# A fused two-block transformer kernel: the order of the down products' matmuls in three of four feed-forward groups

## The chip, the cores and the metric

The kernel runs on one NeuronCore of a Trainium2 chip. The metric is device time in microseconds (us) of one launch; lower is better. The engines run side by side and meet only at semaphores: TensorE multiplies into PSUM, VectorE and ScalarE compute element by element, GpSimd does so on SBUF only, and SyncE issues most of the transfers from HBM. PSUM has eight banks, each of 128 x 512 numbers of 32 bit.

## The reference

Two transformer blocks on 512 tokens of width 1024, one after the other, all in float32. The first one ends in the feed-forward network that this case is about:

```python
def first_block(x, ln1_w, w_in, ..., w_out, ln2_w, w_up, w_down):
...
    h = h + mix @ w_out[l]
    hn = rms_norm(h, ln2_w[l])
    h = h + jnp.square(jax.nn.relu(hn @ w_up[l])) @ w_down[l]
    return h
```

Here `w_up` is 1024 x 4096 and `w_down` 4096 x 1024. The second block (adaptive norms, an mLSTM and an S5 mixer, a gated feed-forward network) starts from its result.

## The kernel before

**Numbers in two parts.** Every matmul operand in float32 is split into a high part and the rest (`hi`, `lo`), and a product is three matmuls into the same bank: hi x hi, hi x lo, lo x hi (lines 445 to 447 and 495 to 497).

**The weight stream.** All weights come in one stream of tiles of 16 blocks of 128 x 128 (1 MB each). SyncE loads a tile into one of two `raw` slots as soon as GpSimd is done with the tile two before it. ScalarE copies it to one of two `whi` slots (line 984) once the last chunk that reads the old tile in that slot is finished: `hi_upto` waits for a semaphore of TensorE. GpSimd then computes `wlo` = `raw` - `whi` in four quarters (line 1504) and counts each in `lo_split`. TensorE waits for `lo_split` before the first use of a quarter. ScalarE, GpSimd and SyncE take the tiles strictly in the order of the stream.

**The feed-forward network.** The 4096 hidden channels go in four groups, `for g, kg in enumerate(FF1_GROUPS)`, of eight blocks of 128 channels each. For each group TensorE first makes eight up products (`gemm("up{g}.{j}")`, line 445 ff., 24 matmuls each, two products from one weight tile), in the two G banks in turn. ScalarE takes each out with a Relu; VectorE squares it and splits it into `Bhi[:, j]` and `Blo[:, j]` (lines 2114 to 2118) and signals `B_ready`. Then comes the down product `token_gemm("dn{g}")`, which adds the group's share to the 512 x 1024 result X. It needs four weight tiles and 192 matmuls of 128 x 512:

- First half: columns 0 to 511. The 512 tokens are four token tiles i = 0 to 3, one sum in one of the four T banks each. Tile one of the weights holds blocks k = 0 to 3 of the channels, tile two k = 4 to 7. The order is block by block: for each k the three matmuls of all four token tiles.
- Second half: columns 512 to 1023, again four sums, in the banks G0, G1, O0, O1, and again two weight tiles. The order is the table `staggered` of pairs (weight tile q, token tile i): 12 matmuls each, three pairs of the first weight tile ahead of the first pair of the second, and the last of the first tile's pairs in fifth place.

When a token tile's sum is done (`done`), VectorE adds the bank to X (`add_token`, line 1591), which frees the bank. A group's up products 0 and 1 use banks G0 and G1, thus they wait for the additions of the sums (half 1, token tiles 0 and 1) before them. The first tile of a half releases its `whi` slot when its last matmul is done (`full_W0`), the second one when the half's last sum is done.

**What else VectorE does there.** In the first three groups it also multiplies rows of the adaptive-norm weights (`adaw`, line 1905, 48 pieces, loaded by SyncE in turn with the weight tiles), and it prepares tables of the S5 mixer in small pieces (`s5_piece`) between the additions of the two halves.

**The other order.** `token_gemm` has a switch `by_rows`. With it the second weight tile of the first half, and both of the second half, run token tile by token tile. Before, the mixer's product in the second block uses it for all of its width, and the last group of the second feed-forward network does.

Of the kernel before, what the change touches and what calls it, by code (L numbers as in the profile page):

```python
# [164 lines left out]
def build(nc, d, out):  # L165
    ctx = ExitStack()
    with ctx:
# [16 lines left out]
        def at(name, shape, off, dt=F32):  # L184
            return nc.alloc_sbuf_tensor_at(name, shape, dt, offset=off)
# [14 lines left out]
        Bhi, Blo = at("Bhi", [P, 8, S], offB, F32R), at("Blo", [P, 8, S], offB + 16384, F32R)  # L200
# [218 lines left out]
        def _(pe):  # L419
# [30 lines left out]
            def gemm(name, hi, lo):  # L450

                ps, where = bank("G")
                done(blocks_of(ps, name, hi, lo, range(CHUNKS[INDEX[name]][1])), name, where)

            def gemm_pair(names):

                two = [bank("G") for _ in names]
                for k in range(DC):
                    pe.wait_ge(sem("A_ready"), T.due("A_ready"))
                    for name, (ps, where) in zip(names, two):  # L460
                        ins = blocks_of(ps, name, Ahi, Alo, [k])
                        if k == DC - 1:
                            done(ins, name, where)
# [8 lines left out]
            def normed_rows(s):  # L472

                eight = {}
                for i in range(NT):
                    pe.wait_ge(sem("norm_rows"), T.due("norm_rows"))
                    for k in range(DC) if i else (0, 1, 4, 5, 6, 7, 2, 3):
                        if i == 0:
                            eight[k] = bank("GGOOTTTT"[k])
                        ps, where = eight[k]  # L480
                        ins = pe.transpose(ps[:, i * P:(i + 1) * P], N[:, i, k * P:(k + 1) * P], ident)
                        if i == NT - 1:
                            done(ins, f"xT{s}.{k}", where)
# [301 lines left out]
            for g, kg in enumerate(FF1_GROUPS):  # L785
                for j in range(kg):
                    if g == 0 and j == 0:
                        gemm_pair(["up0.0", "up0.1"])
                    elif g or j > 1:
                        gemm(f"up{g}.{j}", Ahi, Alo)  # L790
                token_gemm(f"dn{g}", Bhi, Blo, kg, "B_ready")
            normed_rows(2)


# [1937 lines left out]
```

## Time and profile before

| | us |
|---|---|
| median of 3 runs | 1525.86 |
| lowest and highest run | 1524.65, 1527.56 |
| the profiled execution, time | 1520.88 |
| the profiled execution, span from first to last instruction | 1519.1 |
| mean granted TensorE clock in it, of full speed | 0.987 |

The profile is of one execution. Its rows are counted in us from the first instruction; lines are those of the kernel file. A matmul's row gives a modelled duration that overlaps the next matmul's, so what TensorE takes is read from start to start. PE is TensorE's matmuls, PEld its weight loads, DVE is VectorE, ACT is ScalarE, POOL is GpSimd. The first feed-forward network lies between about 340 and 690 us: group 0's down product starts at about 381, group 1's at 478, group 2's at 567 and group 3's at 656 us.

### The profile page before, as it was taken

Reading aid. Unit: us, or ns where it says so; the run is one execution under the profiler, and the core shown is the slowest. Engines: PE = TensorE matmul, PEld = TensorE weight load, DVE = VectorE, ACT = ScalarE, POOL = GpSimd, SP = SyncE. Lnnn points to the kernel's source line nnn. Section 1 sums busy time; section 2 is a strip of 40 time slices with the busy share of each in tenths; the row PEclk is TensorE's granted clock in tenths of the full one; section 3 lists DMA queues with packets and bytes.
Section 4 is the critical chain, followed back from the end, with each engine's and each line's share of the span. In section 5 each row is a group of like instructions: output and inputs, shape, how many; then the busy total and the mean of one; then the engine's idle time right before and its main releaser. Section 6 shows DMA issues by size and latency. Waiting matters only on the chain.

```text
span 1519.1 us, 19247 instructions
## 1 busy us (share of the span) xinstructions
PE 1454.3 (96%) x7136; PEld 1172.8 (77%) x7136; DVE 890.4 (59%) x1454; ACT 566.3 (37%) x742; POOL 685.9 (45%) x520
## 2 busy tenths in 40 slices
PE   6999999999999999998999999999988999999997
PEld 4777766778888787887888777778867888888886
DVE  4773557557857788877491556355675333332357
ACT  5233467443222121225342755544335231332231
POOL 2442145426465455654461424445533445354553
PEclk9999999999999999999899999999998999999999
DMA  7323030025646454233734433243213232223222
GB/s 314 111 70 118 29 112 2 29 92 205 243 161 235 152 194 153 84 111 104 161 127 135 171 112 132 104 181 126 106 46 138 83 111 93 102 83 111 83 83 83
DMA packets 48324, 185.69 MB, mean 122 GB/s; under 512 B 12976, under 2 KB 14256, under 8 KB 33392
## 3 DMA queue, kind: packets, MB, share of 16 engines
q1 hardware_dynamic: 30384, 165.53, 30.8%
q10 hardware_dynamic: 17856, 19.01, 4.5%
q8 instruction: 57, 0.93, 0.2%
q14 instruction: 27, 0.22, 0.0%
HBM read 169.71 MB, written 12.58 MB: 120 GB/s over the span
## 4 chain that ended last, share of the span: by engine, by line
issue 32%; PE 26%; POOL 24%; DVE 2%; ACT 0%; POOLq 0%; DVEq 0%
POOL wlo L1504 23%; PE bank L445 5%; PE bank L446 5%; PE bank L447 5%; PE bank L495 3%; PE bank L497 3%; PE bank L496 3%; PE bank L692 1%; DVE X L2393 0%; PE bank L469 0%; PE bank L763 0%; DVE X L2405 0%; POOL wlo L1512 0%; DVE st L1544 0%; DVE X L1591 0%
## 5 line engine op out<-in xcount | busy, mean ns | idle before, releaser
L1504 POOL TENSOR_TENSOR wlo<-raw,whi 128x512 fp32r<-128x512 f32 x440 | 632.8, 1469 | 763.6 <-ACT whi L984 763.5
L445 PE MATMUL bank<-Ahi,whi 128*128 128x512 f32 x1088 | 437.1, 402 | 14.1 <-DVE Alo L1638 4.4
L446 PE MATMUL bank<-Alo,whi 128*128 128x512 f32 x1088 | 426.8, 392 | 0.0
L447 PE MATMUL bank<-Ahi,wlo 128*128 128x512 f32 x1088 | 426.8, 392 | 0.0
L984 ACT ACTIVATE whi<-raw 128x2048 fp32r<-128x2048 f32 x113 | 216.5, 1916 | 239.9 <-PE bank L497 214.0
L445 PEld LDWEIGHTS bank<-Ahi,whi 128*128 128x128 f32 x1088 | 206.3, 190 | 66.1 <-issue 9.7
L447 PEld LDWEIGHTS bank<-Ahi,wlo 128*128 128x128 f32 x1088 | 206.2, 189 | 44.1
L446 PEld LDWEIGHTS bank<-Alo,whi 128*128 128x128 f32 x1088 | 206.5, 190 | 43.5 <-issue 2.4
L495 PE MATMUL bank<-whi,Bhi 128*128 128x512 f32 x496 | 193.9, 391 | 1.7 <-DVEq L1871 1.7
L497 PE MATMUL bank<-whi,Blo 128*128 128x512 f32 x496 | 193.7, 390 | 0.0
L496 PE MATMUL bank<-wlo,Bhi 128*128 128x512 f32 x496 | 193.5, 390 | 0.0
L495 PEld LDWEIGHTS bank<-whi,Bhi 128*128 128x128 f32 x496 | 93.5, 188 | 21.4 <-issue 1.9
L497 PEld LDWEIGHTS bank<-whi,Blo 128*128 128x128 f32 x496 | 93.4, 188 | 19.6
L496 PEld LDWEIGHTS bank<-wlo,Bhi 128*128 128x128 f32 x496 | 93.5, 189 | 19.4
L2449 DVE TENSOR_SCALAR FG<-GP,par 128x512 f32<-128x512 f32 x22 | 12.9, 585 | 130.5 <-ACT GP L1485 130.5
L1905 DVE CUSTOM_DVE_ANT_0 junk<-adaw,cB 128x1024 f32<-128x1024 f32 x48 | 76.9, 1601 | 21.1 <-DMA adaw<-in_ada 16.1
L1208 ACT ACTIVATE G<-bank 128x512 f32<-128x512 f32 x32 | 19.2, 599 | 123.6 <-PE bank L447 123.5
L2114 DVE TENSOR_TENSOR G<-G 128x512 f32<-128x512 f32 x32 | 36.7, 1147 | 31.5 <-ACT G L1208 31.0
L1521 POOL TENSOR_SCALAR Pr<-Pr,MX,GT 128x384 f32<-128x384 f32 (+3 forms) x64 | 37.3, 594 | 31.8 <-DVE MX L1839 31.7
L1591 DVE TENSOR_TENSOR X<-X,bank 128x512 f32<-128x512 f32 x48 | 33.0, 688 | 29.8 <-PE bank L497 28.3
L1485 ACT ACTIVATE GP<-bank 128x512 f32<-128x512 f32 x22 | 13.2, 599 | 98.5 <-PE bank L447 98.4
L1389 ACT ACTIVATE stage<-bank,par 128x512 f32<-128x512 f32 x32 | 21.9, 684 | 66.1 <-PE bank L447 59.0
(397 smaller groups left out, 1872.8 us busy)
## 6 DMA issues: line engine op xcount, KB each, us to landing
raw<-in_ws SPq DMA_DIRECT2D x113, 1024.0 KB, 5.0
adaw<-in_ada SPq DMA_DIRECT2D x48, 512.0 KB, 4.7
spill<-stage ACTq DMA_DIRECT2D x32, 256.0 KB, 2.0
X<-in_x SPq DMA_DIRECT2D x8, 512.0 KB, 5.9
gates<-spill SPq DMA_DIRECT2D x16, 256.0 KB, 5.4
w1k<-in_w1k SPq DMA_DIRECT2D x1, 2048.0 KB, 15.9
w1v<-in_w1v SPq DMA_DIRECT2D x1, 2048.0 KB, 20.1
XM<-spill ACTq DMA_DIRECT2D x8, 256.0 KB, 3.3
```

What stands on the lines that cost most here:

```text
L445: pe.matmul(ps[:], wh, hi[:, k], start=(k == 0), stop=False)
L446: pe.matmul(ps[:], wh, lo[:, k], start=False, stop=False)
L447: ins = pe.matmul(ps[:], wl, hi[:, k], start=False, stop=(k == kn - 1))
L495: pe.matmul(ps[:], h, wh, start=(k == 0), stop=False)
L496: pe.matmul(ps[:], h, wl, start=False, stop=False)
L497: return pe.matmul(ps[:], l, wh, start=False, stop=stop)
L984: act.activation(whi[n % 2][:], raw[n % RAW][:], ACT.Copy).then_inc(sem("hi_split"), 1)
L1504: pool.tensor_tensor(wlo[slot][:, part], raw[slot][:, part], rd(whi[slot][:, part]), ALU.subtract).then_inc(sem("lo_split"), 1)
L1521: pool.tensor_scalar(Pr[u % RING][:, 0:n], Pr[u % RING][:, 0:n], MX[:, u:u + 1], GT[:, i, g:g + 1], ALU.mult, ALU.mult).then_inc(sem("p_re ...
L1591: ins = tt(x, x, ps[:], ALU.add)
L1905: dve.tensor_tensor_reduce(junk[:], adaw[t % 3][:], cB[:], 1.0, 0.0, ALU.mult, ALU.add, mod[:, t:t + 1]).then_inc(sem("ada_used"), 1)
L2114: tt(r[:], r[:], r[:], ALU.mult).then_inc(sem("dve_step"), 1)
```

## The change

Groups 0, 1 and 2 call the down product with `by_rows`; group 3 does not.

```diff
@@ -788,7 +788,7 @@
                         gemm_pair(["up0.0", "up0.1"])
                     elif g or j > 1:
                         gemm(f"up{g}.{j}", Ahi, Alo)
-                token_gemm(f"dn{g}", Bhi, Blo, kg, "B_ready")
+                token_gemm(f"dn{g}", Bhi, Blo, kg, "B_ready", by_rows=g < 3)
             normed_rows(2)
```

Only TensorE's instructions move. In the second half of group 0's down product, these are the places where bank or weight tile changes, with the waits (bank 0 and 1 are G0 and G1, bank 6 and 7 are O0 and O1; `whi0` is the slot of the half's first weight tile, `whi1` of its second; each row stands for 12 matmuls but the first three of a pair that wait, which stand for 3). Before, on TensorE:

```order
L495 MATMUL bank0<-whi0_51,Bhi_57 128x512 [waits free_O1,free_O0,lo_split,free_G1,free_G0]
...
L495 MATMUL bank1<-whi0_51,Bhi_57 128x512
...
L495 MATMUL bank6<-whi0_51,Bhi_57 128x512
...
L495 MATMUL bank0<-whi1_52,Bhi_57 128x512 [waits lo_split]
...
L495 MATMUL bank7<-whi0_51,Bhi_57 128x512
...
L495 MATMUL bank1<-whi1_52,Bhi_57 128x512
...
L495 MATMUL bank6<-whi1_52,Bhi_57 128x512
...
L495 MATMUL bank7<-whi1_52,Bhi_57 128x512
...
L445 MATMUL bank0<-Ahi_55,whi0_51 128x512 [waits lo_split,free_G0]
```

The same place now:

```order
L495 MATMUL bank0<-whi0_51,Bhi_57 128x512 [waits free_O1,free_O0,lo_split,free_G1,free_G0]
...
L495 MATMUL bank0<-whi1_52,Bhi_57 128x512 [waits lo_split]
...
L495 MATMUL bank1<-whi0_51,Bhi_57 128x512
...
L495 MATMUL bank1<-whi1_52,Bhi_57 128x512
...
L495 MATMUL bank6<-whi0_51,Bhi_57 128x512
...
L495 MATMUL bank6<-whi1_52,Bhi_57 128x512
...
L495 MATMUL bank7<-whi0_51,Bhi_57 128x512
...
L495 MATMUL bank7<-whi1_52,Bhi_57 128x512
...
L445 MATMUL bank0<-Ahi_55,whi0_51 128x512 [waits lo_split,free_G0]
```

The first use of `whi1` has moved from behind 36 matmuls to behind 12, and the last use of `whi0` from the 60th matmul to the 84th of 96; the last two rows are the half's end and the next group's first up product.

In the first half of the same product, with the second weight tile, the banks of the four sums are 3, 4, 5, 2. Before, on TensorE, from that tile's first matmul on:

```order
L495 MATMUL bank3<-whi1_52,Bhi_57 128x512 [waits B_ready,lo_split]
...
L495 MATMUL bank4<-whi1_52,Bhi_57 128x512
...
L495 MATMUL bank5<-whi1_52,Bhi_57 128x512
...
L495 MATMUL bank2<-whi1_52,Bhi_57 128x512
...
L495 MATMUL bank3<-whi1_52,Bhi_57 128x512 [waits B_ready,lo_split]
```

The same place now:

```order
L495 MATMUL bank3<-whi1_52,Bhi_57 128x512 [waits B_ready,lo_split]
L496 MATMUL bank3<-wlo1_54,Bhi_57 128x512
L497 MATMUL bank3<-whi1_52,Blo_58 128x512
L495 MATMUL bank3<-whi1_52,Bhi_57 128x512 [waits B_ready,lo_split]
...
L495 MATMUL bank4<-whi1_52,Bhi_57 128x512
```

The second wait for B and weights comes after 3 matmuls where it came after 12; all four of them now stand in the first token tile's 12 matmuls.

## Rows read from the trace of the kernel before

**Rows 1.** page, part 1: busy time (us), share of the span, instructions

```profile
PE 1454.3 (96%) x7136; PEld 1172.8 (77%) x7136; DVE 890.4 (59%) x1454; ACT 566.3 (37%) x742; POOL 685.9 (45%) x520
```

**Rows 2.** instructions in order of time, TensorE: start, us, engine, line, operation

```profile
391.46 0.39 PE L495 MATMUL bank<-whi,Bhi 128*128 128x512 f32 x1
...
402.34 0.39 PE L495 MATMUL bank<-whi,Bhi 128*128 128x512 f32 x1
...
489.38 0.39 PE L495 MATMUL bank<-whi,Bhi 128*128 128x512 f32 x1
...
512.62 0.50 PE L445 MATMUL bank<-Ahi,whi 128*128 128x512 f32 x1 [1.31 <-DVE X L1591]
...
578.02 0.39 PE L495 MATMUL bank<-whi,Bhi 128*128 128x512 f32 x1
...
601.90 0.50 PE L445 MATMUL bank<-Ahi,whi 128*128 128x512 f32 x1 [1.96 <-DVE X L1591]
```

**Rows 3.** the same view, ScalarE, group 0; idle time before in brackets

```profile
402.60 1.92 ACT L984 ACTIVATE whi<-raw 128x2048 fp32r<-128x2048 f32 x1 [8.96 <-PE bank L497]
...
416.22 1.92 ACT L984 ACTIVATE whi<-raw 128x2048 fp32r<-128x2048 f32 x1 [2.52 <-PE bank L497]
```

**Rows 4.** the same view, GpSimd: four subtractions of one tile in a row

```profile
404.59 5.79 POOL L1504 TENSOR_TENSOR wlo<-raw,whi 128x512 fp32r<-128x512 f32 x4 [4.86 <-ACT whi L984]
...
470.30 7.98 POOL L1504 TENSOR_TENSOR wlo<-raw,whi 128x512 fp32r<-128x512 f32 x4 [4.42 <-ACT whi L984]
...
491.63 5.02 POOL L1504 TENSOR_TENSOR wlo<-raw,whi 128x512 fp32r<-128x512 f32 x4 [5.70 <-ACT whi L984]
...
580.28 5.07 POOL L1504 TENSOR_TENSOR wlo<-raw,whi 128x512 fp32r<-128x512 f32 x4 [5.86 <-ACT whi L984]
...
602.03 5.03 POOL L1504 TENSOR_TENSOR wlo<-raw,whi 128x512 fp32r<-128x512 f32 x4 [1.91 <-ACT whi L984]
```

**Rows 5.** waits, 340 to 720 us: us in total, times, longest

```profile
PE bank L445 <- DVE X L1591: 3.3, 2, 2.0
```

**Rows 6.** in order of time, VectorE, the first feed-forward network

```profile
387.11 1.66 DVE L2118 TENSOR_TENSOR Blo<-G,Bhi 128x512 fp32r<-128x512 f32 x1
...
411.71 2.86 DVE L1591 TENSOR_TENSOR X<-X,bank 128x512 f32<-128x512 f32 x4
...
511.87 2.85 DVE L1591 TENSOR_TENSOR X<-X,bank 128x512 f32<-128x512 f32 x4
...
601.16 2.85 DVE L1591 TENSOR_TENSOR X<-X,bank 128x512 f32<-128x512 f32 x4
...
678.47 0.69 DVE L1591 TENSOR_TENSOR X<-X,bank 128x512 f32<-128x512 f32 x1 [4.06 <-PE bank L497]
```

**Rows 7.** in order of time, the mixer's product, which runs row by row

```profile
1097.38 0.39 PE L495 MATMUL bank<-whi,Ahi 128*128 128x512 f32 x1
...
1108.27 0.39 PE L495 MATMUL bank<-whi,Ahi 128*128 128x512 f32 x1
...
1108.52 1.92 ACT L984 ACTIVATE whi<-raw 128x2048 fp32r<-128x2048 f32 x1 [8.96 <-PE bank L497]
...
1110.52 4.99 POOL L1504 TENSOR_TENSOR wlo<-raw,whi 128x512 fp32r<-128x512 f32 x4 [5.86 <-ACT whi L984]
...
1111.85 0.50 PE L495 MATMUL bank<-whi,Ahi 128*128 128x512 f32 x1 [0.70 <-POOL wlo L1504]
...
1115.57 0.50 PE L495 MATMUL bank<-whi,Ahi 128*128 128x512 f32 x1 [0.27 <-POOL wlo L1504]
```

**Rows 8.** page, part 6: DMA issues, KB each, median us to landing

```profile
raw<-in_ws SPq DMA_DIRECT2D x113, 1024.0 KB, 5.0
```

**Rows 9.** stretches: us, busy of PE, PEld, DVE, ACT, POOL, granted clock, DMA, GB/s

```profile
511.10:512.60 1.50, 0.20 (x1) 0.00 (x0) 1.33 (x6) 1.20 (x1) 0.00 (x0) 1.00 0.62 131
1108.20:1132.50 24.30, 22.77 (x97) 17.56 (x97) 18.16 (x35) 11.27 (x14) 4.99 (x4) 1.00 0.03 13
724.00:734.00 10.00, 10.00 (x64) 9.96 (x64) 7.69 (x5) 2.95 (x4) 9.15 (x5) 0.69 0.38 133
```

## The prediction

> **What bounds the kernel now.** TensorE is busy 96% of the span [rows 1], so I read its own row of time first. In the first feed-forward network its matmuls start 226.7 ns apart: 48 of them lie between 391.46 and 402.34 us, 10.88 / 48 [rows 2]. One weight tile feeds 48 matmuls, so it lasts 10.88 us. The engines behind it have slack: the copy to `whi` takes 1.92 us on ScalarE [rows 3], the four subtractions of `wlo` 5.0 to 8.0 us on GpSimd [rows 4]. The reader is to see in rows 3 and 4 not how long these take but when they may start: `whi` has two slots, and the copy starts 0.26 us after the last matmul that reads the old tile (402.60 against 402.34) [rows 2, 3]. GpSimd begins 1.99 us after the copy did (404.59) [rows 4].
>
> The other thing to see is who keeps TensorE waiting now. In the whole network it waits twice for VectorE's additions to X at an up product [rows 5], for bank G0. Unhindered, the second half of a down product lasts 96 x 0.2267 = 21.76 us. So group 1 would have gone on at 489.38 + 21.76 = 511.14 and went on at 512.62: 1.48 us lost. Group 2: 578.02 + 21.76 = 599.78 against 601.90: 2.12 us lost [rows 2]. Together 3.60 us. VectorE was not waiting for TensorE there. Its four additions run back to back from 511.87 and from 601.16, the first ending at 512.56 and 601.85, because other work of its own came before them [rows 6].
>
> **The change, part by part.** Only TensorE's order changes, in three down products, and no instruction is added or removed.
>
> *First half, second tile.* Block by block becomes token tile by token tile. The waits for blocks 4 to 7 of B and of the weights now fall within 21 matmuls, less than 5 us, instead of 37 matmuls. In group 1 the last quarter of that tile is ready at 470.30 + 7.98 = 478.28 [rows 4], before the tile is begun (489.38 - 10.88 = 478.50). In group 0 the last B ends at 387.11 + 1.66 = 388.77 [rows 6], before 391.46. So this costs nothing: the cover is 0.2 us plus the 9 matmuls (2.04 us) until block 7 is due. Three of four sums are finished up to 8 us sooner, but VectorE begins these additions only at 411.71 in group 0, 9.4 us after the half has ended at 402.34, and is late in the other groups too, where even the second half's additions start after their sums [rows 2, 6]. I put that at nothing.
>
> *Second half, second tile.* Before, three token tiles of the first weight tile (36 matmuls, 8.16 us) stood ahead of the first use of the second. Now 12 matmuls stand there, 2.72 us. The slot of the second tile is freed only at the end of the first half, in both orders, since the last bank of that half ends there. Then block 7 is wanted 12 + 9 = 21 matmuls after the half began, 4.76 us, and is there 0.06 us after GpSimd's pass ends. From rows 2 and 4:
> group 0: 404.59 + 5.79 + 0.06 = 410.44, wanted 402.34 + 4.76 = 407.10, wait 3.34 us;
> group 1: 491.63 + 5.02 + 0.06 = 496.71, wanted 494.14, wait 2.57 us;
> group 2: 580.28 + 5.07 + 0.06 = 585.41, wanted 582.78, wait 2.63 us.
> Together 8.54 us. The kernel has one product in this very order, the mixer's. Its second half starts at 1108.27, ScalarE copies at 1108.52, GpSimd passes from 1110.52 for 4.99 us, and block 7 starts at 1115.57 where 1113.03 was due: 2.54 us late, in four waits [rows 7]. The 0.06 us is from there (1110.52 + 4.99 = 1115.51).
>
> *The next group's first up product.* Its tile takes the slot of the half's first tile, which is released by that tile's last matmul: before after 60 of 96 matmuls (copy at 416.22, and 402.34 + 13.60 = 415.94) [rows 2, 3], now after 84. Then 12 matmuls, 2.72 us, are left. From the release to the first usable quarter the mixer shows 1111.85 - 1108.27 = 3.58 us [rows 7]. Wait 0.86 us, three times 2.58 us. The later quarters come every 1.25 us and are used every 2.72 us. If VectorE shares the pass, a quarter can take 2.0 us (7.98 / 4) instead of 1.25 [rows 4], and each wait is 1.6 us. I take 0.86, because the pass that runs beside the additions at 601.16 takes 5.03 us [rows 4, 6], and these additions are what lies beside it.
>
> *The lost 3.60 us.* TensorE now reaches the next up product at 511.14 + 2.57 = 513.71 and 599.78 + 2.63 = 602.41 on the old scale, after bank G0 was freed at 512.56 and 601.85. Both waits for VectorE vanish. They don't come on top but are replaced: the gain is 3.60 us, and what is late next is the weight tile.
>
> *What else moves.* The third tile after the half is fetched when GpSimd's pass over the up tile ends. That pass ends about 4 us after the up product starts, not before it. The load lands 5.0 us later [rows 8]; with up to 7 us it is there about when its slot comes free (10.88 us), and it is not read for another 10.88 us. Queued behind it on SyncE are loads of `adaw`, which VectorE wants only from the third channel block of the next group on. No cost. In group 3 VectorE's small additions of tables now lie under GpSimd's passes, at most some 4 us of lateness. At the last down product VectorE still waits 4.06 us for TensorE [rows 6]. Nothing to the end, so long as that slack holds.
>
> Sum: 8.54 + 2.58 - 3.60 = 7.5 us. Each wait moves everything behind it, since VectorE's and SyncE's work in the later groups is itself started by TensorE's results. Bounds: at the bottom the mixer's 2.54 for all three groups and 0.86, so 7.6 + 2.6 - 3.6 = 6.6; at the top the up waits at 1.6, so 9.7. The profiled execution has a span of 1519.1 and a time of 1520.9 us. It would become 1526.6 and 1528.4. The median of the runs is 1525.86, some 5 us above that execution, with runs from 1524.65 to 1527.56, so my forecast on the medians' scale is **1533.4 us**.
>
> **A rule weighed.** Block by block, where every third matmul goes on to another bank, loses nothing: matmuls are 226.7 ns apart there, and 10.89 / 48 = 226.9 ns in the mixer's row-by-row half (1097.38 to 1108.27) [rows 2, 7], at a granted clock of 1.00 (2.4 GHz) [rows 9]. The Trainium skill, "TensorE: Matmul & The Clock Gate", section "HAM oscillation — how this bites in real kernels", advises to order the loop so that all blocks of the contraction of one tile run together, which keeps TensorE's clock up. By that rule the change would pay; here the clock is at its upper level already, so by the trace it adds nothing to the sum of 7.5 us, and by the rule alone the sum would be below zero. Its chance is within that of the first rival.
>
> **The rivals.**
> *Faster: earlier banks are what counts.* With the sums done one after another, VectorE frees banks sooner. If the weight tile were there in time, only the -3.60 us would stand: 1522.3 us. It decides at GpSimd's pass: it would have to end 3.34, 2.57 and 2.63 us earlier. Against it: copy and pass start at the release, with 0.26 us and no queue ahead, and the mixer's four waits. The Trainium skill, "Perfetto Trace Analysis", section "Matmuls", says that groups should rotate through banks so that the emptying of one overlaps the matmuls of the next; this speaks for the change, and by it alone one would forecast this rival. Chance 0.04.
>
> *Partly paid back.* A place behind the three groups where TensorE waits for VectorE anyway could swallow delay; the largest such slack that I see is the 4.06 us at the last down product, though there VectorE waits for TensorE [rows 6], which speaks against it. Time: 1533.4 - 4.1 = 1529.3 us. Chance 0.09.
>
> *Longer passes.* Should all GpSimd passes concerned run at 7.98 us, the down waits grow by 2.2 + 3.0 + 2.9 = 8.1 and the up waits by 2.2: 1543.7 us. For it: such passes exist when VectorE multiplies beside them. Against it: at the down product nothing of VectorE's work moves against the pass. Chance 0.09, mostly for a part of it.
>
> *The clock falls.* TensorE will be idle for 2.5 us in four pieces. In one low stretch (724 to 734 us) the granted clock averages 0.69, 3.1 us lost of 10 [rows 9]; three times that is 9.3: 1542.7 us. Against it: in the idle 1.5 us of group 1 and through the mixer's waits the clock stays at 1.00 [rows 9]. Chance 0.03.
>
> *It does nothing.* If the order at run time let the tile through as before, or every wait were hidden, 1525.9 us. Chance 0.03.
>
> **How the numbers follow.** The forecast has 0.72, with a range of its own of 1531 to 1536 (6.6 to 9.7 and some 1 us for the medians). The range 1529 to 1538 takes in the second rival and the start of the third; outside are 0.04 + 0.03 + 0.03 and most of the 0.09 of the long passes, 0.19. About 0.2%, 3 us, is what a measurement of this kernel can tell from no change. Faster by more: 0.04. Within: the rival of no effect and half of the second, 0.08. Slower: 0.88.
>
> **What would show it.** In the profile after: at L495 twelve waits for `wlo`, four in each down product, with block 7 some 2.6 to 3.3 us late; one wait of about 0.9 us for `wlo` at L445 in front of each of the three following groups; no wait of L445 for X at L1591 in groups 2 and 3; matmuls still 227 ns apart; clock 1.00. I am wrong if the second halves last 21.8 us as before, if waits for VectorE remain beside those for GpSimd, if GpSimd's passes there differ from 5.0 to 5.8 us, or if the end moves less than the start of group 3 does.

## The result, and the profile after

| | before | changed kernel |
|---|---|---|
| median of 20 runs each | 1524.41 us | 1529.34 us |
| lowest and highest run | 1517.25, 1527.56 | 1525.04, 1533.78 |
| span of the profiled execution | 1519.1 us | 1527.1 us |

The ratio is 1.0038, with a 95% interval from 1.0026 to 1.0049: the changed kernel is slower by 5.8 us (4.0 to 7.5); the medians alone differ by 4.93. The times here and below are of executions with a mean granted clock of 0.98 to 0.99; two of the twelve of e9 had 0.85 and took 1652 us, and are left out. The forecast was 1533.4 us in a range from 1529 to 1538, worked out as 7.5 us slower. 1529.34 us lies in the range at its lower end. Of the 4.1 us to 1533.4, 1.45 us are the starting point: over 20 runs before has a median of 1524.41, not 1525.86 us. The rest is that the timed difference is smaller than the 7.5 us of the forecast.

TensorE has the same instructions as in [rows 1] and is as busy, part 1 of the page after (busy time, share, instructions):

```profile
PE 1459.3 (96%) x7136; PEld 1173.4 (77%) x7136; DVE 888.6 (58%) x1454; ACT 566.6 (37%) x742; POOL 685.0 (45%) x520
```

**TensorE after, group 1.** In order of time (start, us, engine, line, operation, in brackets the idle time before and who ended it). The second half of the down product begins at 490.67 us.

```profile
490.67 0.39 PE L495 MATMUL bank<-whi,Bhi 128*128 128x512 f32 x1
...
494.25 0.50 PE L495 MATMUL bank<-whi,Bhi 128*128 128x512 f32 x1 [0.70 <-POOL wlo L1504]
...
495.49 0.50 PE L495 MATMUL bank<-whi,Bhi 128*128 128x512 f32 x1 [0.28 <-POOL wlo L1504]
...
496.73 0.50 PE L495 MATMUL bank<-whi,Bhi 128*128 128x512 f32 x1 [0.27 <-POOL wlo L1504]
...
497.97 0.50 PE L495 MATMUL bank<-whi,Bhi 128*128 128x512 f32 x1 [0.26 <-POOL wlo L1504]
...
516.06 0.47 PE L445 MATMUL bank<-Ahi,whi 128*128 128x512 f32 x1 [0.80 <-POOL wlo L1504]
```

These are the waits of the forecast, in number and in place: one for each quarter of the second weight tile, and one ahead of the next up product. Block 7 was due at 490.67 + 4.76 = 495.43 us and starts at 497.97: 2.54 us late. The idle times in brackets count from the modelled end of the matmul before, so they show less than is lost: the second to fourth quarter start 1.24 us apart where three matmuls take 0.68, and the bracket shows 0.28 of these 0.56 us.

**The waits of TensorE after**, from 340 to 730 us (us in total, times, longest); the rows on X of [rows 5] are gone:

```profile
PE bank L495 <- POOL wlo L1504: 4.6, 12, 0.7
PE bank L445 <- POOL wlo L1504: 2.4, 3, 0.8
```

For the same reason these 7.0 us stand for some 11 us of lateness, which is reckoned below from start to start.

**ScalarE and GpSimd after**: the copy behind the start of the second half of group 1, which answers to [rows 3], and the passes of groups 0, 1 and 2, which answer to the first, third and fourth of [rows 4]:

```profile
490.93 1.92 ACT L984 ACTIVATE whi<-raw 128x2048 fp32r<-128x2048 f32 x1 [8.96 <-PE bank L497]
```

```profile
402.12 4.98 POOL L1504 TENSOR_TENSOR wlo<-raw,whi 128x512 fp32r<-128x512 f32 x4 [3.77 <-ACT whi L984]
...
492.92 4.99 POOL L1504 TENSOR_TENSOR wlo<-raw,whi 128x512 fp32r<-128x512 f32 x4 [5.72 <-ACT whi L984]
...
583.69 5.05 POOL L1504 TENSOR_TENSOR wlo<-raw,whi 128x512 fp32r<-128x512 f32 x4 [5.75 <-ACT whi L984]
```

The copy still starts 0.26 us after the release and the pass 1.99 us after the copy. Only group 0's pass is another: 4.98 us where before had 5.79.

**Where the 8.0 us between the spans lie.** The two programs issue the same 113 copies of weight tiles on ScalarE in the same order, so the starts of these copies cut both traces into the same stages. The stretch that holds the change runs from the copy behind the first weight tile of group 0's down product to the copy behind the first half of group 3's. (The down products of groups 1, 2 and 3 start at 467.62, 556.26 and 645.56 us before. The 478, 567 and 656 us given with the time and profile before are the starts of their second weight tiles.) Before:

```profile
391.72 1.92 ACT L984 ACTIVATE whi<-raw 128x2048 fp32r<-128x2048 f32 x1 [8.53 <-PE bank L497]
...
667.58 1.92 ACT L984 ACTIVATE whi<-raw 128x2048 fp32r<-128x2048 f32 x1 [8.96 <-PE bank L497]
```

After:

```profile
389.24 1.92 ACT L984 ACTIVATE whi<-raw 128x2048 fp32r<-128x2048 f32 x1 [8.54 <-PE bank L497]
...
672.54 1.92 ACT L984 ACTIVATE whi<-raw 128x2048 fp32r<-128x2048 f32 x1 [8.96 <-PE bank L497]
```

That is 275.86 us before and 283.30 us after, **7.44 us more**. Ahead of it the changed kernel's execution was 2.48 us ahead, and behind it, between 698 and 1020 us on the old scale, it lost another 3.0 us. Neither is the change's: e10 below, an execution of the kernel before, is 2.40 us ahead at the same place, and e1, whose stretch is hardly delayed, 2.85 us. Behind the stretch e10 loses 4.9 us and e1 2.9. From 1163 us on the distance stays at 8.0 us. I therefore judge all experiments by this stretch, and by the timed ratio beside it.

### The profile page after: what moved, and what is told of

Same layout as the page of the kernel before. It is cut to its first block, busy times and chain, and to the rows that moved or that the text cites. A ratio compares the mean times of both kernels' runs of the same rounds, so it can differ in the third digit from the quotient of the medians.

```text
span 1527.1 us, 19247 instructions
## 1 busy us (share of the span) xinstructions
PE 1459.3 (96%) x7136; PEld 1173.4 (77%) x7136; DVE 888.6 (58%) x1454; ACT 566.6 (37%) x742; POOL 685.0 (45%) x520
## 4 chain that ended last, share of the span: by engine, by line
issue 32%; PE 25%; POOL 24%; DVE 3%; ACT 0%; POOLq 0%; DVEq 0%
POOL wlo L1504 23%; PE bank L445 5%; PE bank L446 5%; PE bank L447 5%; PE bank L495 3%; PE bank L496 3%; PE bank L497 3%; PE bank L692 1%; DVE Alo L1638 0%; DVE X L2393 0%; PE bank L469 0%; PE bank L763 0%; DVE Ahi L1636 0%; DVE X L2405 0%; POOL wlo L1512 0%
## 5 line engine op out<-in xcount | busy, mean ns | idle before, releaser
L1504 POOL TENSOR_TENSOR wlo<-raw,whi 128x512 fp32r<-128x512 f32 x440 | 631.7, 1468 | 772.7 <-ACT whi L984 772.6
L445 PE MATMUL bank<-Ahi,whi 128*128 128x512 f32 x1088 | 436.2, 401 | 12.0 <-DVEq L1577 3.8
L445 PEld LDWEIGHTS bank<-Ahi,whi 128*128 128x128 f32 x1088 | 206.1, 189 | 63.2 <-issue 12.7
L495 PE MATMUL bank<-whi,Bhi 128*128 128x512 f32 x496 | 195.1, 393 | 6.3 <-POOL wlo L1504 4.6
L495 PEld LDWEIGHTS bank<-whi,Bhi 128*128 128x128 f32 x496 | 93.5, 188 | 30.9 <-POOL wlo L1504 9.8
L1591 DVE TENSOR_TENSOR X<-X,bank 128x512 f32<-128x512 f32 x48 | 33.0, 687 | 40.7 <-PE bank L497 39.4
```

Source lines behind the costliest of these rows:

```text
L445: pe.matmul(ps[:], wh, hi[:, k], start=(k == 0), stop=False)
L495: pe.matmul(ps[:], h, wh, start=(k == 0), stop=False)
L1504: pool.tensor_tensor(wlo[slot][:, part], raw[slot][:, part], rd(whi[slot][:, part]), ALU.subtract).then_inc(sem("lo_split"), 1)
L1591: ins = tt(x, x, ps[:], ALU.add)
```

## The experiments

The forecast is one sum of three terms: waits for the second weight tile in the down products (8.5 us), waits for the tile of the next up product (2.6), and waits for VectorE that go (-3.6). The experiments take these terms apart. The table has the stretch against that of before (275.86 us), its three parts (from the copy behind the start of the second half of groups 0, 1 and 2 to a copy within the next group's up products), and the timed ratio with its interval. Unhindered, a group's part is 33.07 us; before is above that by 1.61 us in group 1 and 2.26 in group 2.

| kernel | stretch, us | group 0 | group 1 | group 2 | ratio to before |
|---|---|---|---|---|---|
| changed kernel | +7.44 | +3.77 | +2.12 | +1.56 | 1.0038 [1.0026, 1.0049] |
| e1 first half alone | +0.49 | 0 | +0.03 | +0.46 | 1.0008 [0.9999, 1.0018] |
| e2 second half alone | +7.54 | +3.77 | +2.15 | +1.62 | 1.0046 [1.0029, 1.0063] |
| e3 early use alone | +4.93 | +3.39 | +1.08 | +0.47 | 1.0017 [1.0002, 1.0032] |
| e4 late release alone | -0.61 | +1.09 | -0.53 | -1.17 | 0.9994 [0.9983, 1.0004] |
| e5 before, table pieces behind | -3.86 | 0 | -1.61 | -2.26 | 0.9961 [0.9948, 0.9974] |
| e6 after, table pieces behind | +7.44 | +3.78 | +2.16 | +1.50 | 1.0033 [1.0021, 1.0045] |
| e7 mixer, two pairs ahead | +1.86 | 0 | 0 | +1.85 | 0.9992 [0.9980, 1.0005] |
| e8 e5 and e7 | -3.86 | 0 | -1.61 | -2.26 | 0.9960 [0.9946, 0.9973] |
| e9 release after 72 matmuls | +2.65 | +0.58 | -1.61 | +3.68 | 0.9984 [0.9965, 1.0004] |
| e10 before again | +0.13 | 0 | 0 | +0.12 | one run |
| e11 after again | +7.83 | +4.10 | +2.16 | +1.58 | one run |

**e1 and e2: the two halves apart.** `token_gemm` gets a table of pairs for its second half, so that each half's order can be set alone. e1 keeps the change's first half and gives the second half its old order back:

```diff
-                for q, i in row_by_row if by_rows else staggered:
+                for q, i in pairs or (row_by_row if by_rows else staggered):
...
-                token_gemm(f"dn{g}", Bhi, Blo, kg, "B_ready")
+                token_gemm(f"dn{g}", Bhi, Blo, kg, "B_ready", by_rows=g < 3,
+                           pairs=((0, 0), (0, 1), (0, 2), (1, 0), (0, 3), (1, 1), (1, 2), (1, 3)) if g < 3 else None)
```

> Only the first half of the three down products runs token tile by token tile; the second half keeps its old order. The measure inside one execution is the stretch from ScalarE's whi copy behind the first weight tile of group 0's down product (391.72 us in the profile of before) to the copy at the end of the first half of group 3's (667.58): 275.86 us before, 283.30 us with the whole change. My theory (all of the cost is in the second half): 275.9 us, within 0.3, and the two waits of L445 for X stay at 1.5 and 2.1 us. Rival (the waits for B and weights, drawn together into 21 matmuls, cost something, or the earlier sums let VectorE finish sooner): at least 1 us longer, or shorter by up to 3.6 us with the waits for X gone.

e2 does the reverse:

```diff
+                token_gemm(f"dn{g}", Bhi, Blo, kg, "B_ready",
+                           pairs=((0, 0), (1, 0), (0, 1), (1, 1), (0, 2), (1, 2), (0, 3), (1, 3)) if g < 3 else None)
```

> Only the second half of the three down products runs token tile by token tile. Theory: the stretch from 391.72 to 667.58 us of before (275.86 us) becomes 283.3 us, as with the whole change, with twelve waits for wlo at L495 and three at L445 and none for X. Rival (the first half carries a part): less than 282.5 us.

Measured: e1 +0.49 us, e2 +7.54. The whole of the change's price is in the second half's order. The first half costs next to nothing (0.49 us, where at most 0.3 was expected): e1's two waits for VectorE stand (from 340 to 730 us; the kernels with a table have one line more, so that L1592 and L1505 are L1591 and L1504 of before), the one ahead of group 3 with 2.43 us instead of 1.96 [rows 2], which is its +0.46:

```profile
PE bank L445 <- DVE X L1592: 3.7, 2, 2.4
```

**e3 and e4: early use and late release apart.** In e3 the first pair of the second tile stands in second place, as in the change, but the first tile is released after 60 matmuls as before. In e4 the second tile is used first after 36 matmuls, as before, but the first tile is released after 84.

```diff
+                # e3
+                           pairs=((0, 0), (1, 0), (0, 1), (0, 2), (0, 3), (1, 1), (1, 2), (1, 3)) if g < 3 else None)
+                # e4
+                           pairs=((0, 0), (0, 1), (0, 2), (1, 0), (1, 1), (1, 2), (0, 3), (1, 3)) if g < 3 else None)
```

> The second half in the order (0,0) (1,0) (0,1) (0,2) (0,3) (1,1) (1,2) (1,3): the second weight tile is used after 12 matmuls, as in the change, but the first one is released after 60, as before. Theory: the down waits stand alone, 3 x 2.6 = 7.8 us (8.5 if group 0's pass takes 5.8 us again), less the 3.6 us of waits for bank G0 that they replace: the stretch is 275.86 + 4.2 = 280.1 us (279.8 to 280.9). No wait for wlo at L445. Rival (the early use costs and the waits for VectorE stay on top): 283.7 us.

> The second half in the order (0,0) (0,1) (0,2) (1,0) (1,1) (1,2) (0,3) (1,3): the second tile is used after 36 matmuls, as before, and the first one is released after 84, as in the change. Theory: no wait for wlo at L495; at the next up product the wait is the longer of the weight tile's (1.0 us, as the profile after shows 1.1) and bank G0's (0, 1.5 and 2.1 us), so only group 0 changes: the stretch is 275.86 + 1.0 = 276.9 us. Rival (the waits add up, since the later weight tile also delays VectorE): 275.86 + 3.0 = 278.9 us.

Measured: e3 +4.93 us, within the expected range, and e4 -0.61 us. The waits, from 340 to 730 us, e3:

```profile
PE bank L495 <- POOL wlo L1505: 5.3, 12, 1.4
```

and e4:

```profile
PE bank L445 <- POOL wlo L1505: 2.4, 3, 0.8
```

Each order brings its own wait and not the other's: the two new terms are two mechanisms. But e4's stretch was expected about 1 us longer and is 0.61 shorter. It has no wait for X at all, though its sum in bank G0 is done no earlier within the half than before (after 48 of 96 matmuls). The prediction's account of that wait, VectorE being late on its own work, was right, but that VectorE's work takes the same time in every order was not.

Why is in VectorE's rows. Before, group 1, VectorE prepares a small table (128 x 16) and then adds to X:

```profile
505.70 1.14 DVE L1975 TENSOR_TENSOR s<-pw 128x16 f32<-128x16 f32 x1
506.88 1.21 DVE L1977 TENSOR_TENSOR s<-pw 128x16 f32<-128x16 f32 x1
...
509.37 1.21 DVE L1981 TENSOR_TENSOR s<-pw 128x16 f32<-128x16 f32 x1
...
510.83 0.18 DVE L1975 TENSOR_TENSOR s<-pw 128x16 f32<-128x16 f32 x1
```

and GpSimd, in the same trace, works on the next up tile:

```profile
505.23 5.32 POOL L1504 TENSOR_TENSOR wlo<-raw,whi 128x512 fp32r<-128x512 f32 x4 [8.58 <-ACT whi L984]
```

Four of ten small instructions take 1.2 us instead of 0.18, those that fall under GpSimd's pass (505.23 to 510.55); its instructions are about 1.25 us long. After, with the up tile released later, the pass begins at 514.64 us, behind all ten, and they are quick. VectorE after:

```profile
506.96 0.18 DVE L1975 TENSOR_TENSOR s<-pw 128x16 f32<-128x16 f32 x1
507.17 0.17 DVE L1977 TENSOR_TENSOR s<-pw 128x16 f32<-128x16 f32 x1
...
509.05 2.13 DVE L1591 TENSOR_TENSOR X<-X,bank 128x512 f32<-128x512 f32 x3
...
515.38 0.69 DVE L1591 TENSOR_TENSOR X<-X,bank 128x512 f32<-128x512 f32 x1 [4.20 <-PE bank L497]
```

Against the start of the half the additions come 18.38 us behind (509.05 - 490.67) instead of 22.49 (511.87 - 489.38) [rows 2, 6], and in group 2 19.3 us behind instead of 23.1. So both waits for VectorE do go by the change, but not only because TensorE comes later: VectorE's additions come about 4 us sooner, since its own work got out from under GpSimd's pass. In group 1 of e3, where the waits hold up TensorE and with it the release, the pass is behind this work too. The pass of e4 begins at 509.27 us, when the additions that free G0 and G1 are done:

```profile
507.24 2.13 DVE L1592 TENSOR_TENSOR X<-X,bank 128x512 f32<-128x512 f32 x3
```

By these rows the two engines take turns: a small instruction waits for the end of a large one of the other. The Trainium skill, "SBUF — State Buffer", section "Who interferes with whom", says that VectorE and GpSimd share one pair of ports, held by one of them at a time, and that an instruction of VectorE with two SBUF inputs, like these of L1975 to L1981, contends with one of GpSimd that reads SBUF. The trace agrees: 1.2 us is one GpSimd instruction, not a share of one. The additions to X have one input in PSUM and are not slowed (0.69 to 0.71 us each, under a pass or not), as the page would have it.

**e5 and e6: what the waits for VectorE are worth.** The small table pieces are moved behind the additions, e5 in the kernel before, e6 in the changed one:

```diff
-                for n in [(), (5,), (10, 11)][g]:
-                    s5_piece(n)
                 for i in range(NT):
                     add_token(f"dn{g}", 1, i)
-                for n in [(), (), (12, 13)][g]:
+                for n in [(), (5,), (10, 11, 12, 13)][g]:
```

> The kernel before, but in groups 1 and 2 VectorE prepares the tables of the S5 mixer (pieces 5, and 10 and 11) behind the additions of the second half instead of between the halves. Theory (VectorE frees G0 late because of its own work, not because the sums come late): TensorE's waits of 1.5 and 2.1 us for X at L445 vanish and the stretch from 391.72 to 667.58 us of before, 275.86 us, becomes 272.3 us; the kernel is about 3.6 us or 0.24% faster. Rival (the sums come too late, and the change's order is what frees the bank): the waits stay and the stretch is 275.9 us.

> The changed kernel with the same move of VectorE's pieces. Theory: with the change the weight tile is last and bank G0 is free in time, so nothing is gained: the stretch stays at 283.3 us, that is 11.0 us more than with the pieces moved alone, which is the full price of the new order with no saving against it (3 x 2.6 down waits and 3 x 1.1 up waits). Rival (bank G0 still holds the up product in part): up to 2 us less than 283.3 us.

e5 is a faster kernel than before by 0.39% (1518.15 us median). VectorE now waits for TensorE's sums instead of the other way round. Group 1 of e5, in order of time, VectorE and GpSimd:

```profile
505.90 0.69 DVE L1591 TENSOR_TENSOR X<-X,bank 128x512 f32<-128x512 f32 x1 [1.15 <-PE bank L497]
508.62 0.69 DVE L1591 TENSOR_TENSOR X<-X,bank 128x512 f32<-128x512 f32 x1 [2.03 <-PE bank L497]
...
510.60 0.17 DVE L1977 TENSOR_TENSOR s<-pw 128x16 f32<-128x16 f32 x1
510.81 1.15 DVE L1979 TENSOR_TENSOR pw<-s 128x16 f32<-128x16 f32 x1
```

```profile
510.61 5.07 POOL L1504 TENSOR_TENSOR wlo<-raw,whi 128x512 fp32r<-128x512 f32 x4 [2.41 <-ACT whi L984]
```

The same table work goes from 0.17 to 1.15 us at the moment when the pass begins, where nobody waits for it now. e6 gains nothing on the changed kernel (+7.44 against +7.44): there these waits were already gone. So e6 over e5 is the full price of the new waits, 11.30 us in the stretch, and e5 shows what was lost before, 3.86 us. By the ratios it is 1.0033 / 0.9961 = 1.0072, or 11.0 us, which agrees.

**e7 and e8: the same order in the mixer's product.** If waits for the weight tile cost there too, a table with two pairs of the first tile ahead of the second should give them back [rows 7]. e7 is the kernel before with it, e8 has e5's edit too.

```diff
-            token_gemm("mix", Ahi, Alo, 8, "A_gated", by_rows=True)
+            token_gemm("mix", Ahi, Alo, 8, "A_gated", by_rows=True,
+                       pairs=((0, 0), (0, 1), (1, 0), (1, 1), (0, 2), (1, 2), (0, 3), (1, 3)))
```

> The kernel before, with the second half of the mixer's product in the order (0,0) (0,1) (1,0) (1,1) (0,2) (1,2) (0,3) (1,3): 24 matmuls stand ahead of the second weight tile, where 12 did. Theory (a wait for the pass of GpSimd that ends 7.24 us after the half began, block 7 wanted after 24 + 9 matmuls, 7.48 us): the four waits for wlo vanish, the mixer's half is 2.5 us shorter, and all behind it comes 2.5 us sooner, 0.16%. Rival (the following norm waits for VectorE and ScalarE, not for the sums): the waits vanish but the norm's transposes start no sooner, 0 us.

> The kernel before with both: VectorE's pieces behind the additions, and two token tiles ahead in the mixer. Theory: the two gains are in different places and add up, 3.6 + 2.5 = 6.1 us or 0.40% faster than before. Rival (only the first holds): 3.6 us.

The waits for `wlo` are gone, but the mixer's stage is shorter by only 0.97 us (e8: 0.98), not 2.5, and of that 0.81 (e8: 1.03) remains a stage later. What is late next is VectorE, with additions, statistics and norms for each row. e7:

```profile
1121.75 0.69 DVE L1594 SCALAR_TENSOR_TENSOR X<-X,bank 128x512 f32<-128x512 f32 x1 [4.11 <-PE bank L497]
...
1126.48 0.69 DVE L1594 SCALAR_TENSOR_TENSOR X<-X,bank 128x512 f32<-128x512 f32 x1
...
1131.61 0.69 DVE L1594 SCALAR_TENSOR_TENSOR X<-X,bank 128x512 f32<-128x512 f32 x1
```

The second and third addition begin without idle time before them, 5.13 us apart, where TensorE makes a sum in 24 x 0.2267 = 5.44 us. VectorE's work on a row is nearly as long as TensorE's, so it makes up little when the sums come sooner. The timed runs can't tell e7 from no change, nor e8 from e5.

**e9: a table that should keep both gains.** Two pairs ahead of the second tile, and the release after 72 matmuls:

```diff
+                           pairs=((0, 0), (0, 1), (1, 0), (1, 1), (0, 2), (0, 3), (1, 2), (1, 3)) if g < 3 else None)
```

> The second half of the first three down products in the order (0,0) (0,1) (1,0) (1,1) (0,2) (0,3) (1,2) (1,3): 24 matmuls ahead of the second tile, and the first tile released after 72 of 96. Theory: no wait for wlo at L495 (block 7 is wanted 7.48 us after the half began and GpSimd's pass ends 7.24 to 7.3 us after it), none at L445 (24 matmuls, 5.44 us, are left and the tile needs 3.6 to 3.7), and GpSimd's pass over the next group's first up tile starts 2.7 us later than before, so that it no longer lies on VectorE's small table operations and bank G0 is free in time. The stretch from 391.72 to 667.58 us of before, 275.86 us, becomes 272.0 us, as with VectorE's pieces moved, without moving them. Rival (VectorE's lateness is its own work whatever GpSimd does): waits for X of 1.6 and 2.3 us stay, 275.9 us.

The stretch is 278.51 us where 272.0 was expected. Group 1 came as expected (-1.61), groups 0 and 2 did not. In group 0 GpSimd's pass took 5.62 us, and block 7 was 0.45 us late. In group 2 the release 12 matmuls later leaves GpSimd's pass on the table work of that group, and four of its small instructions are slow where before had three. e9, VectorE:

```profile
592.67 1.26 DVE L2054 TENSOR_TENSOR ctab<-ctab,dbl 128x16 f32<-128x16 f32 x1
...
594.06 1.17 DVE L2049 TENSOR_TENSOR dbl<-stab,pw 128x32 f32<-128x32 f32 x1
...
597.94 2.85 DVE L1592 TENSOR_TENSOR X<-X,bank 128x512 f32<-128x512 f32 x4
```

GpSimd and TensorE, e9:

```profile
592.59 5.16 POOL L1505 TENSOR_TENSOR wlo<-raw,whi 128x512 fp32r<-128x512 f32 x4 [11.27 <-ACT whi L985]
```

```profile
598.68 0.80 PE L445 MATMUL bank<-Ahi,whi 128*128 128x512 f32 x1 [2.74 <-DVE X L1592]
```

The additions are late again and the wait is 2.74 us. Behind it the granted clock fell; stretches of e9 (us; busy time of PE, PEld, DVE, ACT, POOL; granted clock; DMA share; GB/s):

```profile
598.60:602.00 3.40, 3.32 (x8) 2.64 (x9) 3.26 (x6) 0.00 (x0) 3.40 (x4) 0.50 0.84 294
602.00:606.00 4.00, 4.00 (x14) 3.13 (x13) 3.12 (x11) 0.00 (x0) 1.01 (x1) 0.65 0.47 131
```

At 0.50 TensorE runs at 1.2 instead of 2.4 GHz. The up product 3.0 was taken out 8.6 us after its start instead of 5.8 before, so the clock cost about 3 us of group 2's part, as much as the wait. This is one execution: the timed ratio, 0.9984, has e9 no slower than before, so its other executions can hardly have lost as much.

**e10 and e11: before and after once more.** They show how far one execution speaks.

> The kernel before once more, for a second profile of it. Theory (the waits for bank G0 in groups 1 and 2 depend on how VectorE's work falls against GpSimd's passes and the loads of adaw, so they vary): the stretch is 275.86 us to 278 us. Rival (they are fixed): 275.9 us within 0.1.

> The changed kernel once more. Theory (no wait for VectorE is left in it, only waits behind GpSimd's passes): the stretch is 283.3 us within 0.1, or up to 0.8 us more if group 0's pass over the second tile takes 5.8 us instead of 5.0. Rival (the same spread as in the kernel before): up to 2 us off.

e10 has +0.13 us in the stretch, e11 +7.83, 7.70 apart. I had expected that before itself varies by 2 us in group 2, since e7, whose first network is unchanged, had +1.85 there; e10 doesn't show it. e11's stretch, 283.69 us, is within what was expected. Both e7 and e10 wait for VectorE ahead of group 3's up products. e7:

```profile
602.31 0.50 PE L445 MATMUL bank<-Ahi,whi 128*128 128x512 f32 x1 [2.20 <-DVE X L1592]
```

```profile
602.00:606.00 4.00, 3.69 (x10) 2.92 (x11) 3.86 (x7) 0.12 (x1) 3.81 (x4) 0.61 0.62 246
```

e10:

```profile
599.61 0.50 PE L445 MATMUL bank<-Ahi,whi 128*128 128x512 f32 x1 [2.06 <-DVE X L1591]
```

```profile
602.00:606.00 4.00, 4.00 (x19) 3.30 (x18) 3.93 (x10) 0.59 (x1) 2.67 (x3) 1.00 0.17 33
```

After 2.20 us of idle time the clock fell to 0.61 over 4 us, after 2.06 us it stayed at 1.00, and so it did in e1 after 2.43 us. Of e7's +1.85 us the longer wait is 0.24, the rest is this fall.

## Why the prediction was right, point by point

**The kind and the place of the loss: right.** Twelve waits at L495 and three at L445, all for `wlo`, none for X. e3 and e4 show them as two separate mechanisms, e2 has the whole loss, e1 next to none of it. Matmuls stay 227 ns apart otherwise, and the granted clock over 340 to 730 us is 1.00.

**Waits in the down products: 8.54 us put, 7.7 found.** Block 7 starts 2.5 us late in group 0 (407.15 against 399.86 + 4.76), 2.5 in group 1, 2.6 in group 2. The latter two were put at 2.57 and 2.63. Group 0 was put at 3.34, since its pass had taken 5.79 us [rows 4]. I took that for the pass's length at this place. It is the length of an undisturbed pass, 4.98 us, and, less 0.1 us, what was left of an instruction of VectorE on `adaw` when the pass began:

| execution | VectorE's instruction on `adaw` ends after the pass begins by | pass, us |
|---|---|---|
| after | 0.11 us | 4.98 |
| e4 | 0.28 | 5.18 |
| e11 | 0.44 | 5.29 |
| e1 | 0.58 | 5.47 |
| e9 | 0.72 | 5.62 |
| e10 | 0.77 | 5.67 |
| e3 | 0.84 | 5.70 |
| before | 0.91 | 5.79 [rows 4] |

A few tenths of a us in when `adaw` lands decide it: VectorE waits for a load of it just before. And e3, with the early use of the change, had 5.70 us and lost 3.3 us there, as forecast. The better price for group 0 was the 5.02 us of group 1's row in [rows 4]; the odd one among the three rows at this place needed a reason before it could be carried over.

**Waits ahead of the up products: 2.58 us put, 3.3 found.** In group 1 the up product was due at 490.67 + 21.76 + 2.54 = 514.97 and starts at 516.06, 1.09 us late (groups 0 and 2: 1.13 and 1.09). It was put at 0.86. About 0.1 of the rest comes from block 7's matmul, which starts again after a wait: its row is 0.50 us instead of 0.39, and the next one starts 0.34 us on (407.15, 407.49) instead of 0.227. The sum had no term for this restart. The other 0.13 is the way from the release to the first quarter, 3.7 instead of the mixer's 3.58 us: the release was due at 490.67 + 2.54 + 0.1 + 84 x 0.2267 = 512.35. The bound of 1.6 us, with VectorE in the pass, was not reached.

**The waits that go: -3.60 us put, -3.87 found** (e5's groups 1 and 2; again 0.1 us of restart each). The prediction has them vanish because TensorE comes later, which would have left group 1 free by 1.15 us and group 2 by 0.56. That reason was not needed: VectorE is about 4 us earlier. The prediction had taken VectorE's additions to stay where they were against the half. It asked what VectorE does to GpSimd's pass over the next up tile, not what that pass does to VectorE. That step was wrong; that it erred on the harmless side was luck. e9 shows the other side of the same coupling, a release that is moved by 2.7 us and leaves a wait of 2.74 us in group 2.

**The sum: 7.5 us put, 7.44 found in the stretch.** It is 11.3 - 3.9 where 11.1 - 3.6 was put. The misses are -0.9 (group 0's pass for the most part), +0.7 (up waits), +0.3 (three restarts behind the up waits) and -0.3 (more was lost before), which nearly cancel. The timed difference is 5.8 us (4.0 to 7.5), the interval's end being just where the stretch is; e2 and e6, in other executions, have 7.0 (4.4 to 9.6) and 5.0 (3.2 to 6.9). The interval doesn't rule out that the two agree. But in all the kernels timed, apart from e1 and e7, which keep before's waits for VectorE, the timed difference lies below the stretch's, by 0.3 us (e4) to 5 (e9). One candidate is the clock: e7 lost 1.6 us by it behind the wait ahead of group 3's up products, which before has as well, and of the four executions with this wait that were profiled (before, e1, e7, e10) one fell. If it falls in some of before's timed executions too, the stretch of the profiled one, 275.86 us, is too short as a measure of before. No run here shows that it does. Single executions also differ by some us in regions that no edit touches, as at 185 us and from 698 us on.

**The rivals.** *Faster by earlier banks*: banks are freed earlier, and e4 and e5 show what that is worth, 3.9 us at most; the weight tile isn't there in time. *Partly paid back*: its 1529.3 us is almost the measured median, but that is chance, since the starting point was lower and its mechanism isn't there. VectorE's wait for the last down product is as long as before, 4.06 us in [rows 6]:

```profile
683.44 0.69 DVE L1591 TENSOR_TENSOR X<-X,bank 128x512 f32<-128x512 f32 x1 [4.07 <-PE bank L497]
```

and from 1163 us on the delay stands unchanged. Between the stretch and the end, the executions with a long stretch (after, e2, e3, e6, e11) lose another 2.3 to 4.9 us against before's, and e1, e4, e5, e9 and e10 lose 0.3 to 4.9: no delay of several us is given back. *Longer passes*: 4.98 to 5.05 us in after, not 7.98. *The clock*: it stayed at 1.00 in both executions of the changed kernel; it did fall behind single waits of 2.2 and 2.7 us in e7 and e9, so the mechanism is there, but in two executions of the changed kernel the waits in four short pieces did not set it off. The rule that was weighed, on keeping a tile's blocks of the contraction together, would have had the change pay; it did not, as the rows on matmul distance said. The Trainium skill, "TensorE: Matmul & The Clock Gate", section "HAM oscillation — how this bites in real kernels", gives that advice for thin-M kernels (few rows for each block of weights), in which TensorE waits for DMA at every block. The prediction left this condition out, and this product doesn't meet it: before, TensorE waits in it for no DMA.

## What to carry to other kernels

A reordered loop has two dates for each double-buffered operand: when it is first used after its slot came free, and when it is released for the next. Work both out from the release to the first usable piece (here 3.6 us, then 1.25 us a piece) before counting what earlier results bring. Where one engine waits for another that is busy with its own work, move that work behind the hand-over first (e5, -0.39%), and look at which of the third engine's instructions lie on it, since they may be what makes it slow.

## What the runs showed of the hardware that I had not expected

- VectorE's small instructions with two SBUF inputs take 0.17 to 0.20 us alone and mostly 1.14 to 1.28 us beside a GpSimd subtraction of 128 x 512 (1.25 us). In group 2, where up to four such instructions in a row don't wait for each other, every second one is slow (e9: 1.17, 0.18, 1.27, 0.18 us). In turn, a GpSimd pass that begins under a VectorE instruction on `adaw` is longer by what is left of that one less 0.1 us (0.11 to 0.91 us gave 0 to 0.81 us). L1983 of this table work, with one SBUF input, was slowed too when it fell under a pass (1.21 us in e5).
- A matmul of 128 x 512 that starts after a wait delays its successor by about 0.1 us.
- The granted clock fell to 0.50 and 0.61 behind single waits of 2.74 and 2.20 us (e9, e7), and stayed at 1.00 behind ones of 1.96, 2.06 and 2.43 us at the same place (before, e10, e1), so the length of the wait alone doesn't decide it. Where it fell, it cost about 1.6 us (e7) and 3 us (e9). What else decides it stays open.
